# GpSimd forms the last token tile's gated sum, and the last tile is scaled and stored in two halves

## The reference

```python
gate_w = top_vals / top_vals.sum(-1, keepdims=True)        # two gates per token
...
y_slots = y_buf[dest].reshape(N, TOP_K, D)                 # two expert rows per token
return jnp.einsum('nk,nkd->nd', gate_w.astype(x2d.dtype), y_slots)
...
x = layer_norm(ALPHA * x + m.reshape(B, S, D), ln_ffn_g[l], ln_ffn_b[l])
```

## Time and profile before

| | |
|---|---|
| median of 3 runs | 881.12 us (880.66 to 881.78) |
| the profiled execution, its own time | 882.18 us |
| its span in the profile | 880.4 us |
| TensorE busy | 849.6 us (96%) |
| VectorE busy | 407.0 us (46%) |
| GpSimd busy | 58.7 us (7%) |
| mean granted TensorE clock | 0.986 |

### The profile page before, as it was taken

How to read it: one execution, slowest core, us unless ns; L and a number is a source line. 1 busy time by engine, 2 the same in 40 slices (tenths; PEclk the granted TensorE clock), 3 DMA queues, 4 the chain that set the end, 5 groups by cost and what they waited for, 6 DMA issues and landing times.

```text
span 880.4 us, 16470 instructions
## 1 busy us (share of the span) xinstructions
PE 849.6 (96%) x7102; PEld 494.0 (56%) x7102; DVE 407.0 (46%) x666; ACT 256.4 (29%) x463; POOL 58.7 (7%) x74
## 2 busy tenths in 40 slices
PE   9999999999999999999897999999999999999996
PEld 7889788777888878733232463556533333333332
DVE  5588867777586584783221133120021212212237
ACT  6223535354358331530312111211122210211212
POOL 2200000000000000001020100000010000000203
PEclk9999999999999999999997999999999999999998
DMA  9822131313213249989999999999999999999992
GB/s 357 330 96 96 51 141 48 144 49 120 96 49 143 96 177 404 422 337 372 402 397 393 397 417 415 413 401 408 398 419 382 421 396 408 416 406 409 422 371 104
DMA packets 43560, 258.06 MB, mean 293 GB/s; under 512 B 5450, under 2 KB 5598, under 8 KB 18272
## 3 DMA queue, kind: packets, MB, share of 16 engines
q1 hardware_dynamic: 37440, 239.16, 68.5%
q0 software_dynamic: 6048, 17.86, 5.4%
HBM read 245.93 MB, written 13.42 MB: 295 GB/s over the span
## 4 chain that ended last, share of the span: by engine, by line
PE 78%; DMA 7%; DVE 6%; ACT 4%; issue 3%; SPq 1%; POOL 0%; POOLq 0%; DVEq 0%; ACTq 0%
PE ps L1093 21%; PE ps L731 10%; PE ps L732 9%; PE ps L736 9%; PE ps L1116 9%; PE ps L1104 6%; PE ps L1139 4%; DMA raw_e<-in_expert_w_gate_up 3%; DMA yt<-yd 2%; PE ps L1153 1%; ACT sc L1414 1%; DMA norm_rows<-in_ln_ffn_b 1%; PE ps L778 1%; PE ps L1076 1%; DMA yd<-ye,sidx 1%
## 5 line engine op out<-in xcount | busy, mean ns | idle before, releaser
L1093 PE MATMUL ps<-raw_e,xt_strip 128*32 128x512 f32 x1888 | 207.8, 597 | 0.1
L1093 PEld LDWEIGHTS ps<-raw_e,xt_strip 128*32 128x32 f32 x1888 | 61.0, 111 | 140.3 <-issue 138.6
L2098 DVE TENSOR_TENSOR strip<-strip,ps 64x1536 f32<-64x1536 f32 (+2 forms) x18 | 24.2, 1343 | 212.3 <-ACT strip L1541 212.3
L731 PE MATMUL ps<-xh,hi_m 128*128 128x512 f32 x272 | 108.0, 397 | 0.0
L732 PE MATMUL ps<-xl,hi_m 128*128 128x512 f32 x272 | 106.2, 391 | 0.0
L1541 ACT ACTIVATE strip<-ps 64x1536 f32<-64x1536 f32 (+2 forms) x18 | 20.0, 1111 | 256.1 <-PE ps L1093 188.7
L1116 PE MATMUL ps<-raw_e,hT 128*32 128x512 f32 x752 | 85.1, 595 | 0.0
L1672 DVE SCALAR_TENSOR_TENSOR cacc<-hg,cwt,cacc 128x512 f32<-128x512 f32 x120 | 82.2, 745 | 0.0
L1640 DVE TENSOR_TENSOR lo_m<-raw_m,hi_m 128x2048 fp32r<-128x2048 f32 x27 | 61.9, 2291 | 42.8 <-ACT hi_m L1362 42.6
L1104 PE MATMUL ps<-raw_e,xt_strip 128*32 128x256 f32 x1280 | 69.8, 379 | 1.3 <-DMA raw_e<-in_expert_w_gate_up 1.3
L736 PE MATMUL ps<-xh,lo_m 128*128 128x512 f32 x272 | 67.2, 389 | 0.0
(11 more groups left out here) (326 smaller groups left out, 934.7 us busy)
## 6 DMA issues: line engine op xcount, KB each, us to landing
raw_e<-in_expert_w_gate_up SPq DMA_DIRECT2D x126, 1024.0 KB, 21.3
raw_e<-in_expert_w_down SPq DMA_DIRECT2D x60, 1024.0 KB, 21.7
raw_m<-in_w_in_chunks SPq DMA_DIRECT2D x20, 1024.0 KB, 5.1
yd<-zeros POOLq DMA_DIRECT2D x8, 512.0 KB, 7.0
raw_m<-in_w_o SPq DMA_DIRECT2D x4, 1024.0 KB, 5.4
yt<-yd SPq DMA_DIRECT2D x4, 1024.0 KB, 14.9
front<-in_front_rows SPq DMA_DIRECT2D x3, 768.0 KB, 7.3
raw_m<-in_w_conv_out SPq DMA_DIRECT2D x2, 1024.0 KB, 5.4
```

The lines of the kernel that those rows point to most:

```text
L731: pe.matmul(dst, a1, b1, start=first, stop=False)
L1093: mm = pe.matmul(ps[at_, bank + g], xt[:, c, g * STRIP:(g + 1) * STRIP], cols[s], start=(c == 0), stop=(c == GU - 1))
```

## The change

GpSimd waits for tile 3's rows, multiplies each of the two by its gate (read as one column, repeated 1024 times), waits for both, and adds them in place. TensorE waits for this sum and adds it to PSUM with the identity as weights: one product in place of two. VectorE no longer makes the two gate diagonals of tile 3. The three new GpSimd operations stand in its queue ahead of the additions for tiles 0 to 2. The final scaling of tile 3 is done in two halves of 512 columns, and each half is stored when it is ready.

```diff
@@ SyncE
-            for t in range(NT):
-                if t < NT - 1:
-                    sp.wait_ge(fin_ready, t + 1)
-                else:
-                    sp.wait_ge(fin_last, 1)
+            for t in range(NT - 1):
+                sp.wait_ge(fin_ready, t + 1)
                 sp.dma_start(out_v[t], ot[t]).then_inc(out_st, 16)
-            sp.wait_ge(out_st, 16 * NT)
+            for half in range(2):
+                cols = slice(half * 512, (half + 1) * 512)
+                sp.wait_ge(fin_last, half + 1)
+                sp.dma_start(out_v[NT - 1][:, cols], ot[NT - 1][:, cols]).then_inc(out_st, 16)
+            sp.wait_ge(out_st, 16 * (NT + 1))
@@ GpSimd
+            pool.wait_ge(token_in[NT - 1], 16)
+            for k in range(2):
+                gate = gwt[:, k, NT - 1:NT].to_broadcast([P, D])
+                pool.tensor_tensor(yt[NT - 1][:, k], yt[NT - 1][:, k], gate, ALU.mult).then_inc(rows_summed, 1)
+            pool.wait_ge(rows_summed, 2)
+            pool.tensor_tensor(yt[NT - 1][:, 0], yt[NT - 1][:, 0], yt[NT - 1][:, 1], ALU.add).then_inc(rows_summed, 1)
             pool.wait_ge(lnf_sb, 1)
             for t in range(NT - 1):
                 pool.wait_ge(fin_s, t + 1)
@@ TensorE
+                elif t == NT - 1:
+                    pe.wait_ge(rows_summed, 3)
+                    add_rows(t, yt[t][:, 0], ident)
@@ VectorE
-                    for t in range(PRESUM, NT):
+                    for t in range(PRESUM, NT - 1):
                         ins = dve.tensor_scalar(gate_diag[:, k, t], ident, gwt[:, k, t:t + 1], None, ALU.mult)
...
-            scale(NT - 1, ot[NT - 1], lnf, lgv, frstd, fin_last)
+            for half in range(2):
+                cols = slice(half * 512, (half + 1) * 512)
+                scale(NT - 1, ot[NT - 1][:, cols], lnf[:, :, cols], lgv, frstd, fin_last)
```

More of the change, by code:

```diff
@@ L415, in build @@
         pool_set, norm_bc, lnf_sb = sem("pool_set"), sem("norm_bc"), sem("lnf_sb")
+        rows_summed = sem("rows_summed")
         idv, sel_blk, idx_mm = (sem(n) for n in ("idv", "sel_blk", "idx_mm"))
```

## The result

The changed kernel takes 885.77 us (median of 5 runs, 882.83 to 888.11) against 881.12 us (5 runs, 880.21 to 882.07). The ratio, worked out from all the runs and not from the medians alone, is 1.0050, with a 95% interval of 1.0027 to 1.0074: 2.4 to 6.5 us slower. The forecast was 884.9 us, in a range of 882.5 to 886.8. The profiled execution took 885.79 us at a span of 884.1 us, so the spans differ by 3.7 us.

What follows compares the result with a forecast made beforehand. The end was taken as bound by TensorE, then VectorE, then one 512 KB store. VectorE's holding adds 4.30 us, halving gives back 0.5; 881.12 + 3.8 = 884.9 us, range 882.5 to 886.8.

Steps and rivals of the forecast that it cites:

- The sign and the mechanism: Slower by 3.8 us: GpSimd's three new operations and the additions queued behind them hold VectorE's two-tensor operations.
- the two stretched rows of line 1650: VectorE's 128x1 operation before the change, tiles 1 and 2: each ends with a GpSimd addition; maximum 770 ns, median 220.
- Line 1654 is held too: VectorE's next two-SBUF-tensor operation, assumed held like line 1650; in tile 0 until the second multiplication ends at 867.07 us.
- Rival 2: On VectorE only line 1650 is held, not line 1654: 2.2 us later after the store, 883.3 us; chance 0.10.
- rival 1: The second multiplication, following without a wait, keeps line 1650 of tile 0 held until 867.07: +5.0 us, 886.1; chance 0.15.
- The mis-sized term: Each GpSimd multiplication of tile 3's rows by its gate, taken at 2.35 us from line 725's addition.
- F0: GpSimd's addition for tile 0, queued behind the new operations: forecast to start at 869.52 us instead of 864.77.
- rival 3: GpSimd's multiplications are cheap, near 0.98 us each: 882.2 us, decided below 1.33 us each; chance 0.07.
- TensorE's end of tile 3: TensorE waits for GpSimd's sum, then ends tile 3 at 872.55 us, against 872.39 before.
- Each tile's cycle on VectorE: End of line 1654 from tile to tile under GpSimd's additions: 872.27, 876.28, 880.29 us, the last 4.30 later than before.
- Rival 4: GpSimd does not hold VectorE in the new places; the stores queue up: +0.6 us, 881.7; chance 0.10.
- Rival 5: Faster: VectorE starts tile 3 at best 0.86 us sooner, plus 0.6 us in the store; chance 0.02.

Runs made afterwards that it cites:

- one_tensor: Changed kernel with both two-tensor Newton operations (lines 1650 and 1654) given one SBUF tensor and a per-partition scalar; 879.98 us, ratio 0.9983 to the kernel before.
- side: Kernel before plus GpSimd's three new operations, writing to a spare buffer nobody reads, TensorE keeping both gate products; 884.78 us, ratio 1.0037.
- side_fill: Kernel before plus six GpSimd fills of 128x1024, which read nothing, in the queue place of the three new operations; 882.73 us, ratio 1.0016.
- one_tensor_1650: Changed kernel with only line 1650's operation on one SBUF tensor, line 1654's left on two; 882.09 us, ratio 1.0008 to the kernel before.
- sum_only: Changed kernel without the halves: GpSimd forms tile 3's sum, the last tile is scaled and stored whole; 886.18 us, ratio 1.0051 to the kernel before.
- early_rows: Changed kernel with both Newton operations on one SBUF tensor and tile 3's rows read back ahead of tile 2's; 880.56 us, ratio 0.9981 to the kernel before.
- one_tensor_again: Repeat of the changed kernel with both Newton operations on one SBUF tensor; 880.77 us, ratio 0.9993 to the kernel before.

## Why the prediction was right

- *The sign and the mechanism* were right, and stood in the two stretched rows of line 1650. That each was held by GpSimd is now shown by three experiments: the loss goes when the operations read one tensor (one_tensor), stays when nobody uses GpSimd's result (side), and the holding is absent under fills (side_fill).
- *Line 1654 is held too*, which no row had shown: 1.63 us in tile 0, ending with the second multiplication. Rival 2 falls, and one_tensor_1650 confirms it from the other side.
- *Two GpSimd instructions back to back* let line 1661 through between them (865.06 us, first multiplication's end 865.03), so rival 1 falls for this place. Each held operation in these traces waits for the one instruction that is running when it comes.
- *The mis-sized term* is the multiplication by a repeated gate: 1.88 us against the 2.35 taken from the addition with two full inputs. F0 waits for both, so the sum had 2 x 0.47 = 0.94 us too much. With 1.88 it gives 3.8 - 0.9 = 2.9 us, and the tail measured 2.8. It lay about midway between the 2.35 us that was taken and the 1.33 us at which rival 3 would have won. The run doesn't say whether the repeated column makes it cheaper, or that it is a multiplication and line 725 an addition: no multiplication with two full inputs was run.
- *The rest of the sum held.* TensorE's end of tile 3: 872.43 us at a start 0.9 us later than before, so 1.0 us earlier than worked out (872.55), as the multiplications were shorter. That 872.43 and 872.55 lie so close is luck: the later start and the shorter multiplications cancel. Each tile's cycle on VectorE: 4.00 us (871.88 to 875.88, 875.88 to 879.88), 4.01 worked out. The two halves of the scaling took 1.41 us, not 1.30.
- *Rival 4* (nothing is held) is what one_tensor builds. It was worked out at 0.6 us more, and the tail fell by 0.6 us; the shorter multiplications, which bring TensorE's end and F0 0.94 us forward, account for most of that. *Rival 5* needed that nothing is held too.
- *The total* came closer than its terms deserve. With the multiplication at its measured price the sum would have given 884.0 us (881.12 + 2.9), and 885.77 was measured. The median rose by 4.65 us (interval 2.4 to 6.5), of which the tail explains 2.8. The traces show no step before the tail that goes with the change; its start scatters by 3 us between kernels. Whether a part of the 4.65 us is a further cost in front of the tail stays open; the interval does not ask for one, though that of sum_only, 3.3 to 5.7 us, lies just above its tail's 3.15 us. Against one speak the four other kernels with GpSimd's sum. By their ratios they lie 1.5 and 0.6 us below the kernel before (one_tensor and its repetition), 0.7 above (one_tensor_1650) and 1.7 below (early_rows), and their tails alone give 0.6 and 0.5 below, 0.6 above and 0.9 below.

## What to carry to other kernels

Before giving elementwise work to GpSimd, list what VectorE does at that time and look for operations that read two SBUF tensors, and don't pass over the smallest ones: here operations of 128x1, 0.16 to 0.22 us by themselves, were held until the running GpSimd instruction that reads SBUF ended, for up to 1.6 us each. Larger ones were not tried under such an instruction in the tail. A stretch of such a row that ends with a GpSimd row shows it in the profile before anything is changed. Where the second operand is one number per partition, hand it over as a per-partition scalar, which freed the 128x1 operations here; and ask what is queued behind the new work on GpSimd, because it moves too and holds VectorE at new places.

## What the runs showed of the hardware that was not expected

- A GpSimd multiplication of 128x1024 whose second input is one column repeated took 1.88 us, against 2.35 us for an addition with two full inputs. Which of the two differences makes it cheaper was not tried.
- Per-partition scalar operands in SBUF did not bring the holding: 0.27 and 0.21 us under running GpSimd operations, in all four tiles of one_tensor and of one_tensor_again.
- Six GpSimd fills of 128x1024 back to back took 5.41 us, 0.90 each, where a single one had taken 0.98, and held no VectorE operation with two SBUF inputs.
- Of two operations of GpSimd that follow without a wait, the second did not keep a held VectorE operation out: line 1661 of tile 0 ended at 865.06 us, the first multiplication at 865.03 us.
- The two 256 KB halves of the last store landed 2.0 us after their issue with the 512 KB store 1.9 us ahead of them, and 2.5 us with it 0.8 us ahead.
